# Two weight units interleaved at the start of a two-layer encoder kernel on one Trainium2 core

## The chip, the cores and the metric

The kernel runs on one core of one Trainium2 chip. The core has TensorE (PE, matrix products into PSUM), VectorE (DVE), ScalarE (ACT), GpSimd (POOL) and SyncE (SP, which here only issues transfers). The metric is the device time of one execution in microseconds. Three runs of the kernel before gave a median of 1763.88 us, from 1763.88 to 1764.26.

## The reference

The program is a two-layer encoder on 512 tokens of width 1024, everything in float32. For each layer it computes

```python
x = x + hybrid_mixer(rms_norm(x, norm_mix_g[l]), w_in[l], ...)        # 3 branches, gates, w_out
x = x + mem_cross_attention(rms_norm(x, norm_xattn_g[l]), mem, ...)
x = x + conv_ffn(rms_norm(x, norm_ffn_g[l]), w_up[l], ..., w_down[l])
```

and at the end one more `rms_norm`. The mixer multiplies the normed x by a wide `w_in`. Its first 1024 columns feed a branch that gates them (`a * sigmoid(b)`) and runs a causal convolution of 31 taps over them; other columns feed a differential attention and a gated branch, in which a causal 128x128 matrix `w_s` mixes tokens and a bias `b_s` is added. `rms_norm(x)` is `x * rsqrt(mean(x * x) + eps) * g`.

## The kernel before, in words

All activations lie transposed: 128 features on the partitions, 8 tiles of them (`KD`), 512 tokens along the free side. Every large product is done in split precision. A float32 operand is rounded to a "head" of TensorE's float32r type, and the "tail" is the operand minus its head. A product is then head*head + tail*head + head*tail, three matmuls of 128x128 by 128x512 for each block.

The weights come in "units" of 128x2048 floats (1 MB), 78 for a layer, laid out on the host in the order of use. A unit is loaded by SP into `raw[:, g % 2]`, its head is written by ACT (or for a few pieces by DVE) into `w_hd[:, g % 2]`, and its tail by POOL or DVE into `w_tl[:, g % 2]`. Two slots exist, so unit g + 2 waits for unit g. A unit of the kinds used first ("ab") holds 8 blocks of 256 columns, two output tiles (t = 0, 1) for each input tile `kc`. Its 48 matmuls collect in a pair of PSUM banks.

The order of the work is written out by hand, one program for each engine. An engine runs its list in order, and a counter for each engine (`line.done`, `line.at`) carries the waits between them. Labels name the steps: `n0_head{t}` and `n0_tail{t}` are the two parts of x tile t times the gain `g_mix`; `of_unit("head", g)`, `("tail", g)` are the parts of unit g; `("used", g)` says that `w_hd` of unit g was read, `("over", g)` that its last matmul was done; `ev{e}` says that DVE or ACT has emptied the PSUM banks of entry e.

The norm is not applied before the products. The gains are folded into x, and the factor of each token, `rsqrt(mean square)`, is multiplied in when the PSUM banks are emptied. So the first products can start before the norm is known. The factor is made like this: ACT squares the 8 tiles of x (`n0_sq{t}`) into `sq`, which has two places; DVE adds them up in `ssum` (`first_sum`, 7 additions in a row, the last labelled `n0_all`); PE turns `ssum` with 4 transposes (`turned_sums`); DVE reduces it and adds eps (`mean_square`, `n0_ms`); POOL takes the power -0.5 (`n0_rs`); PE spreads the result over the partitions with 4 transposes (`spread`, `n0b`); DVE copies it into `r0` (`n0_r`). In this order each addition waits for its square, and each square from the third on waits for the addition that frees its place.

At the start, PE first runs 14 matmuls on a tile of ones. Then it works through unit 0 in two halves of four input tiles (lines 1508, 1513 and 1522), then unit 1 (lines 1532, 1533 and 1542). Between the head matmuls of unit 1 and its 16 tail matmuls stand `first_sums`: 4 matmuls (lines 1418, 1419) that sum the columns of `w_s` for both layers, and the 4 transposes of `ssum` (line 1398). After unit 1 comes the spread (line 1406), then unit 2. POOL prepares `w_s` for those column sums: it masks it (line 573) and splits it into head and tail (lines 577, 579), after both `w_s` and `b_s` have landed. DVE uses the column sums in 8 small operations (line 997, `bs{lay}_{g}`).

The loads at the start are all issued by SP in one row: x tiles 0-1, first half of unit 0, x 2-3, second half of unit 0, x 4-5, x 6-7, unit 1, `w_st` (that is `w_s`), `b_s`, the other vectors, the identity.

## Time and profile of the kernel before

| what | value |
|---|---|
| median of 3 runs | 1763.88 us |
| the profiled execution, its own time | 1764.1 us |
| its span (first to last instruction) | 1762.3 us |
| PE busy | 1753.0 us, 99% |
| PE weight loads busy | 1452.8 us, 82% |
| DVE busy | 1244.2 us, 71% |
| ACT busy | 730.7 us, 41% |
| POOL busy | 483.7 us, 27% |
| granted TensorE clock over the span | 0.999 |
| the chain that ended last | 98% PE |

The profiled execution lies 1.8 us above its span, since something lies before the first and after the last instruction that is recorded. Busy shares are averages; the change touches only about the first 35 us, so what matters are rows of that stretch. Times in rows count from the start of the span.

### The profile page before, as it was taken

What the parts mean: (1) busy time and instruction counts of PE and PEld (TensorE: products, weight loads), DVE (VectorE), ACT (ScalarE), POOL (GpSimd) and SP (SyncE); (2) the same over time, 40 slices, a digit from 0 to 9 for tenths busy, and PEclk for the clock granted to TensorE, in tenths of its full rate; (3) what the DMA queues carried; (4) which work ended last, traced back from release to release, by engine and by line L of the source; (5) the groups of instructions that cost most, each with busy time, mean ns of one, the idle gap of its engine ahead of it and who ended that gap; (6) DMA issues with size and microseconds to landing.
All of it is one profiled execution on the core that took longest, in us unless ns stands there. A gap on an engine that the chain in (4) does not pass through costs nothing.

```text
span 1762.3 us, 21613 instructions
## 1 busy us (share of the span) xinstructions
PE 1753.0 (99%) x8152; PEld 1452.8 (82%) x8152; DVE 1244.2 (71%) x1656; ACT 730.7 (41%) x940; POOL 483.7 (27%) x201
## 2 busy tenths in 40 slices
PE   9999999999999999999999999999999999999998
PEld 7888888888878888888888888888888788888888
DVE  7987856563568786577779678555744797685586
ACT  5233644343464433343432246443444544343342
POOL 6453000103014244444133620010030232444440
PEclk9999999999999999999999999999999999999999
DMA  5532222322222322232332312223222223322322
GB/s 216 190 120 72 102 102 83 133 96 96 96 96 96 120 99 93 96 113 81 118 143 72 143 65 109 103 95 120 96 96 96 96 96 120 117 75 96 120 73 71
DMA packets 30120, 185.95 MB, mean 106 GB/s; under 512 B 3644, under 2 KB 5948, under 8 KB 9536
## 3 DMA queue, kind: packets, MB, share of 16 engines
q1 hardware_dynamic: 27804, 172.71, 27.4%
q0 software_dynamic: 1648, 11.54, 1.7%
q8 instruction: 64, 1.05, 0.2%
q10 hardware_dynamic: 564, 0.33, 0.1%
q14 instruction: 40, 0.33, 0.1%
HBM read 179.25 MB, written 7.68 MB: 106 GB/s over the span
## 4 chain that ended last, share of the span: by engine, by line
PE 98%; DVE 1%; DMA 1%; issue 0%; ACT 0%; SPq 0%; DVEq 0%; POOL 0%; ACTq 0%
PE ps L1542 28%; PE ps L1532 28%; PE ps L1533 28%; PE ps L1448 2%; PE ps L1440 2%; PE ps L1439 2%; PE ps L1570 1%; PE ps L1590 1%; PE ps L1622 1%; PE ps L1604 1%; DMA raw<-units 1%; DVE ssum L931 1%; PE ps L1582 0%; PE ps L1708 0%; PE ps L1714 0%; PE ps L1707 0%
## 5 line engine op out<-in xcount | busy, mean ns | idle before, releaser
L1532 PE MATMUL ps<-x_hd,w_hd 128*128 128x512 f32 x1584 | 619.5, 391 | 0.0
L1533 PE MATMUL ps<-x_tl,w_hd 128*128 128x512 f32 x1584 | 617.2, 390 | 0.0
L547 POOL TENSOR_TENSOR w_tl<-raw,w_hd 128x2048 fp32r<-128x2048 f32 x80 | 370.0, 4625 | 534.9 <-ACT w_hd L652 396.9
L652 ACT ACTIVATE w_hd<-raw 128x2048 fp32r<-128x2048 f32 (+1 forms) x156 | 298.4, 1913 | 343.2 <-PE ps L1533 258.9
L1542 PE MATMUL ps<-x_hd,w_tl 128*128 128x512 f32 x1584 | 377.3, 390 | 0.0
L1532 PEld LDWEIGHTS ps<-x_hd,w_hd 128*128 128x128 f32 x1584 | 297.4, 188 | 62.5 <-issue 0.3
L1533 PEld LDWEIGHTS ps<-x_tl,w_hd 128*128 128x128 f32 x1584 | 297.6, 188 | 61.1
L1542 PEld LDWEIGHTS ps<-x_hd,w_tl 128*128 128x128 f32 x1584 | 297.1, 188 | 61.5
L1532 PE MATMUL ps<-ring_hd,w_hd 128*128 128x512 f32 (+1 forms) x640 | 242.1, 382 | 0.0
L1533 PE MATMUL ps<-ring_tl,w_hd 128*128 128x512 f32 (+1 forms) x640 | 240.0, 379 | 0.0
L900 DVE TENSOR_TENSOR w_tl<-raw,w_hd 128x2048 fp32r<-128x2048 f32 x75 | 172.0, 2293 | 51.8 <-ACT w_hd L652 40.4
L1231 DVE SCALAR_TENSOR_TENSOR merged<-merged 128x512 f32<-128x512 f32 x44 | 183.0, 4160 | 21.3 <-ACT merged L652 20.9
L1097 DVE TENSOR_TENSOR resid<-resid,ps 128x512 f32<-128x512 f32 x120 | 77.1, 684 | 115.9 <-PE ps L1542 112.6
L1041 DVE SCALAR_TENSOR_TENSOR ps<-cg,pv_all,ps 128x512 f32<-128x512 f32 x232 | 154.5, 750 | 0.0
L1542 PE MATMUL ps<-ring_hd,w_tl 128*128 128x512 f32 (+1 forms) x640 | 151.5, 379 | 0.0
L1532 PEld LDWEIGHTS ps<-ring_hd,w_hd 128*128 128x128 f32 x640 | 120.3, 188 | 29.3 <-issue 4.3
L1533 PEld LDWEIGHTS ps<-ring_tl,w_hd 128*128 128x128 f32 x640 | 120.4, 188 | 22.7 <-issue 0.5
L1542 PEld LDWEIGHTS ps<-ring_hd,w_tl 128*128 128x128 f32 x640 | 116.0, 188 | 22.4
L652 ACT ACTIVATE ring_hd<-merged 128x512 fp32r<-128x512 f32 x44 | 27.9, 633 | 224.9 <-DVE merged L1233 224.9
L1222 DVE SCALAR_TENSOR_TENSOR merged<-tmp,pv_all,merged 128x510 f32<-128x510 f32 (+1 forms) x176 | 120.3, 745 | 0.9 <-ACT merged L652 0.9
L652 ACT ACTIVATE merged<-tmp,pv_all 128x512 f32<-128x512 f32 x88 | 71.9, 817 | 117.3 <-DVE tmp L1211 113.2
L1211 DVE TENSOR_TENSOR tmp<-ps,sq 128x512 f32<-128x512 f32 x88 | 56.7, 686 | 82.0 <-PE ps L1542 81.4
(198 smaller groups left out, 1522.0 us busy)
## 6 DMA issues: line engine op xcount, KB each, us to landing
raw<-units SPq DMA_DIRECT2D x155, 1024.0 KB, 4.8
resid<-x_t SPq DMA_DIRECT2D x4, 512.0 KB, 7.9
bias_t<-bias_tiles POOLq DMA_DIRECT2D x8, 256.0 KB, 5.3
cg<-mem_t POOLq DMA_DIRECT2D x2, 1024.0 KB, 6.3
resid<-x_t POOLq DMA_DIRECT2D x1, 2048.0 KB, 8.2
resid_dram<-resid POOLq DMA_DIRECT2D x1, 2048.0 KB, 7.5
resid<-resid_dram POOLq DMA_DIRECT2D x1, 2048.0 KB, 8.8
out<-resid SPq DMA_DIRECT2D x7, 256.0 KB, 2.3
```

The source lines that it names most:

```text
L547: line.done(pool.tensor_tensor(w_tl[:, k % 2, :], raw[:, k % 2, :], w_hd[:, k % 2, :].bitcast(F32), ALU.subtract), of_unit("tail", g))
L652: line.done(act.activation(out, in_, func, **kw), *labels)
L900: op(lambda: dve.tensor_tensor(w_tl[:, slot, :], raw[:, slot, :], w_hd[:, slot, :].bitcast(F32), ALU.subtract), of_unit("tail", g), needs= ...
L1041: op(lambda: dve.scalar_tensor_tensor(dst, src, w, acc, ALU.mult, ALU.add), independent=1)
L1097: op(lambda: dve.tensor_tensor(dst, dst, ps[:, banks(e) + i, :], ALU.add), f"{tag}_{j + i}", f"ev{e}", needs=(f"e{e}",), independent=i)
L1211: op(lambda: dve.tensor_tensor(src, ps[:, b + i, :], r_all, ALU.mult), f"up_src{arg}_{i}", f"ev{e}", needs=(f"e{e}",), independent=i)
L1222: op(lambda: dve.scalar_tensor_tensor(dst[:, sh:S], src[:, 0:S - sh], col(l, "ffn_w", 3 * c + 2 - sh), dst[:, sh:S], ALU.mult, ALU.add), f ...
L1231: op(lambda: dve.scalar_tensor_tensor(th, th, 1.0, ft[:, f0, :], ALU.add, ALU.mult), needs=(f"th_f{arg}",))
L1439: pe.matmul(ps[:, b + t, :], xh[:, kc, a], w, start=kc == 0, stop=False)
L1532: pe.matmul(dst, w_hd[:, slot, w], hd[:, src, :], start=kc == 0, stop=False)
L1533: i = pe.matmul(dst, w_hd[:, slot, w], tl[:, src, :], start=False, stop=False)
L1542: i = pe.matmul(dst, w_tl[:, slot, w], hd[:, src, :], start=False, stop=kc == nk - 1)
```

## The change

Units 0 and 1 are now worked on together. PE takes a pair of input tiles, does its 12 matmuls for unit 0 (4 head, 4 x-tail, 4 weight-tail) and the same for unit 1, then goes to the next pair. The very first tile of unit 0 is done alone. The loads are cut finer: x comes in five parts (tiles 0, 1, 2-3, 4-5, 6-7), each of the two units in three steps (512, 512 and 1024 columns), in the order of use. DVE now rounds all heads of unit 0, ACT all of unit 1, and DVE makes all six tails, each for one step. The squares of x go to the eight tiles of `merged`, so no square waits for an addition. The 14 matmuls on ones become 9. `first_sums` moves to the last pair of unit 0, with 16 matmuls of the two units behind it as before; the column sums of layer 1 use bank 6 in place of 5. The spread moves into unit 2, behind its first 8 matmuls. POOL's work on `w_s` waits for `w_st` alone, and `b_s` has a semaphore of its own.

PE from its first matmul, before:

```order
L1413 MATMUL ps<-ones 128x128 x14
L1508 MATMUL ps<-x_hd,w_hd 128x512 x4
L1513 MATMUL ps<-x_tl,w_hd 128x512 x4
L1508 MATMUL ps<-x_hd,w_hd 128x512 x4
L1513 MATMUL ps<-x_tl,w_hd 128x512 x4
L1522 MATMUL ps<-x_hd,w_tl 128x512 x8
```

PE from its first matmul, now (1566 multiplies heads, 1572 x tails, 1578 weight tails):

```order
L1451 MATMUL ps<-ones 128x128 x9
L1566 MATMUL ps<-x_hd,w_hd 128x512 x2
L1572 MATMUL ps<-x_tl,w_hd 128x512 x2
L1578 MATMUL ps<-x_hd,w_tl 128x512 x2
L1566 MATMUL ps<-x_hd,w_hd 128x512 x2
L1578 MATMUL ps<-x_hd,w_tl 128x512 x2
L1572 MATMUL ps<-x_tl,w_hd 128x512 x2
L1566 MATMUL ps<-x_hd,w_hd 128x512 x4
L1572 MATMUL ps<-x_tl,w_hd 128x512 x4
L1578 MATMUL ps<-x_hd,w_tl 128x512 x4
```

The first matmuls need one x tile and a quarter of unit 0; the last three rows are unit 1 with the same two x tiles.

PE around the sums and the spread, before (1418, 1419 are the column sums, 1398 turns `ssum`, 1406 spreads, 1532 on the last row is unit 2):

```order
L1418 MATMUL ps<-ring_hd,ones 128x512
L1419 MATMUL ps<-ring_tl,ones 128x512
L1418 MATMUL ps<-ring_hd,ones 128x512
L1419 MATMUL ps<-ring_tl,ones 128x512
L1398 MATMUL ps<-ident,ssum 128x128 x4
L1542 MATMUL ps<-x_hd,w_tl 128x512 x16
L1406 MATMUL ps<-ident,rs 128x128 x4
L1532 MATMUL ps<-x_hd,w_hd 128x512
```

The same place now (1542 and 1543 are unit 2, of whose 8 matmuls ahead of the spread the first two stand; the spread, line 1444, comes behind all 8):

```order
L1457 MATMUL ps<-ring_tl,ones 128x512
L1436 MATMUL ps<-ident,ssum 128x128 x4
L1578 MATMUL ps<-x_hd,w_tl 128x512 x4
L1566 MATMUL ps<-x_hd,w_hd 128x512 x4
L1572 MATMUL ps<-x_tl,w_hd 128x512 x4
L1578 MATMUL ps<-x_hd,w_tl 128x512 x4
L1542 MATMUL ps<-x_hd,w_hd 128x512
L1543 MATMUL ps<-x_tl,w_hd 128x512
```

The transposes of `ssum` have 16 matmuls behind them in both, but the spread has moved behind 8 more.

DVE from x tile 2 to the additions, before:

```order
L924 SCALAR_TENSOR_TENSOR x_tl<-resid,pv_all,x_hd 128x512 x2
L954 TENSOR_TENSOR w_tl<-raw,w_hd 128x1024
L924 SCALAR_TENSOR_TENSOR x_tl<-resid,pv_all,x_hd 128x512 x4
L954 TENSOR_TENSOR w_tl<-raw,w_hd 128x1024
L900 TENSOR_TENSOR w_tl<-raw,w_hd 128x2048
L931 TENSOR_TENSOR ssum<-sq 128x512
L931 TENSOR_TENSOR ssum<-ssum,sq 128x512 x6
```

DVE over the same stretch now:

```order
L952 SCALAR_TENSOR_TENSOR x_tl<-resid,pv_all,x_hd 128x512
L978 CAST w_hd<-raw 128x512
L952 SCALAR_TENSOR_TENSOR x_tl<-resid,pv_all,x_hd 128x512
L983 TENSOR_TENSOR w_tl<-raw,w_hd 128x512 x2
L952 SCALAR_TENSOR_TENSOR x_tl<-resid,pv_all,x_hd 128x512 x2
L978 CAST w_hd<-raw 128x1024
L983 TENSOR_TENSOR w_tl<-raw,w_hd 128x1024
L952 SCALAR_TENSOR_TENSOR x_tl<-resid,pv_all,x_hd 128x512 x2
L983 TENSOR_TENSOR w_tl<-raw,w_hd 128x1024
L960 TENSOR_TENSOR ssum<-merged 128x512
L960 TENSOR_TENSOR ssum<-ssum,merged 128x512 x6
```

The seven additions stand last in both lists, and ahead of them DVE has more and smaller pieces.

The diff, cut to its core:

```diff
-NORM_AT = (1, 0)
-X_PARTS = ((0, 2), (2, 4), (4, 6), (6, 8))
+NORM_AT = (0, 0)
+SPREAD_AT = (2, 1)
+X_PARTS = ((0, 1), (1, 2), (2, 4), (4, 6), (6, 8))
 PIECE = UNIT // 4
+SUMS_AT = (4, 6)
+STEPS = (slice(0, PIECE), slice(PIECE, 2 * PIECE), slice(2 * PIECE, UNIT))
...
+            def load_step(n, p):
+                done = weights_in[n] if p == 2 else piece_in[n][p]
+                sp.dma_start(raw[:, n, STEPS[p]], units[n][:, STEPS[p]]).then_inc(done, 16)
+
             load_x(0)
+            load_step(0, 0)
             load_x(1)
+            load_step(1, 0)
             load_x(2)
+            load_step(0, 1)
+            load_step(1, 1)
             load_x(3)
+            load_step(0, 2)
+            load_x(4)
+            load_step(1, 2)
             sp.dma_start(v_sb[:, 0:DEPTH, :], w_st).then_inc(ws_in, 16)
+            sp.dma_start(ident[:], ident_in).then_inc(ident_loaded, 16)
...
-                    pool.wait_ge(ws_in, 16 * 2)
+                    pool.wait_ge(ws_in, 16)
...
+            first_tiles((0, 1))
+            second_unit(0)
+            squares_of_x((0,))
+            first_tiles((2, 3))
+            second_unit(1)
+            squares_of_x((1, 2))
+            first_tiles((4, 5))
+            squares_of_x((3,))
+            first_tiles((6, 7))
+            second_unit(2)
+            squares_of_x((4, 5, 6, 7))
...
-            for _ in range(14):
+            for _ in range(9):
                 pe.matmul(ps[:, 5, 0:P], ones[:], ones[:], start=True, stop=True)
...
+                pe.wait_ge(vector_done, line.at("step_head0_0"))
+                heads(0, (0,))
+                rests(0, (0,))
+                tails(0, (0,), 0)
+                heads(0, (1,))
+                tails(0, (1,), 0)
+                rests(0, (1,))
+                for j in range(4):
+                    kcs, p = (2 * j, 2 * j + 1), min(j, 2)
+                    for n in (0, 1) if j else (1,):
+                        pe.wait_ge(scalar_done if n else vector_done, line.at(f"step_head{n}_{p}"))
+                        heads(n, kcs)
+                        i = rests(n, kcs)
+                        if j == 3:
+                            line.done(i, of_unit("used", n))
+                        if (j, n) == (3, 0):
+                            first_sums()
+                        i = tails(n, kcs, p)
+                        if j == 3:
+                            line.done(i, f"e{FIRST_OF[n]}", of_unit("over", n))
...
                     if g == 2:
-                        pe.wait_ge(vector_done, line.at(f"bs{DEPTH - 1}_3"))
+                        pe.wait_ge(vector_done, line.at("bs0_3"))
...
-                                first_spread if l and k == NORM_AT[l] + 1 else None)
+                                first_spread if k == SPREAD_AT[l] else None)
...
-                    if k == NORM_AT[l] and not l:
-                        first_spread()
```

`heads`, `rests` and `tails` each run over the input tiles `kcs` and both output tiles, waiting for `n0_head{kc}`, `n0_tail{kc}` and `step_tail{n}_{p}`. In layer 1 the sums and the spread stay where they were.

## Rows read from the trace of the kernel before

**Rows 1.** Waits of PE over the whole span, the longest: us in total, times, longest.

```profile
PE ps L1508 <- DVE w_hd L950: 1.2, 1, 1.2
```

**Rows 2.** Chain of waits, 0 to 80 us: start us, us, what.

```profile
17.28 2.30 DVE w_tl L900
19.68 0.95 DVE ssum L931
...
21.32 0.91 DVE ssum L931
22.33 1.61 DVE ssum L931
...
26.76 0.70 DVE ssum L931
...
28.30 0.66 PE ps L1398 x4
28.96 3.64 PE ps L1542 x16
32.60 0.44 PE ps L1406 x4
...
72.96 3.63 PE ps L1542 x16
```

**Rows 3.** Timeline of the start, PE: start us, us, engine, line, operation, [idle before].

```profile
1.09 4.98 PE L1413 MATMUL ps<-ones 128*128 128x128 f32 x28 [1.09 <-POOL ones L558]
...
7.31 1.19 PE L1508 MATMUL ps<-x_hd,w_hd 128*128 128x512 f32 x4 [1.23 <-DVE w_hd L950]
```

**Rows 4.** Timeline of the start, ACT and DVE.

```profile
5.13 1.54 ACT L652 ACTIVATE x_hd<-resid,pv_all 128x512 fp32r<-128x512 f32 x2 [1.77 <-DMA pv_all<-pvec]
...
6.82 0.43 DVE L950 CAST w_hd<-raw 128x512 fp32r<-128x512 f32 x1
...
8.67 1.54 ACT L652 ACTIVATE x_hd<-resid,pv_all 128x512 fp32r<-128x512 f32 x2 [2.01 <-DMA resid<-x_t]
...
11.10 1.22 DVE L954 TENSOR_TENSOR w_tl<-raw,w_hd 128x1024 fp32r<-128x1024 f32 x1
...
12.30 3.20 DVE L924 SCALAR_TENSOR_TENSOR x_tl<-resid,pv_all,x_hd 128x512 fp32r<-128x512 f32 x4
```

**Rows 5.** Timeline of the start, SP's issue of `w_st` and POOL's work on it.

```profile
4.67 0.66 SPq L476 DMA_DIRECT2D v_sb<-w_st  x1
...
17.88 3.24 POOL L573 TENSOR_SCALAR_AFFINE_SELECT v_sb<-v_sb 128x512 f32<-128x512 f32 x2 [2.98 <-DMA v_sb<-bs]
...
21.76 1.62 POOL L579 TENSOR_TENSOR ring_tl<-v_sb,ring_hd 128x512 fp32r<-128x512 f32 x1
...
24.48 1.62 POOL L579 TENSOR_TENSOR ring_tl<-v_sb,ring_hd 128x512 fp32r<-128x512 f32 x1
```

**Rows 6.** Transfers issued in 0 to 60 us: KB each, median us to landing.

```profile
v_sb<-w_st SPq DMA_DIRECT2D x1, 512.0 KB, 11.6
```

**Rows 7.** Groups of PE, 3.5 to 4 us, then 5.5 to 6.2 us: busy us, mean ns.

```profile
L1413 PE MATMUL ps<-ones 128*128 128x128 f32 x4 | 1.1, 421 | 0.0
...
L1413 PE MATMUL ps<-ones 128*128 128x128 f32 x6 | 0.8, 275 | 0.0
```

**Rows 8.** Timelines of DVE (28 to 100 us) and POOL (26 to 180 us).

```profile
33.07 0.69 DVE L1106 COPY r<-ps 128x512 f32<-128x512 f32 x1 [0.77 <-PE ps L1406]
...
38.13 4.37 DVE L1126 SCALAR_TENSOR_TENSOR cg<-tmp,cg 128x512 f32<-128x512 f32 x1
...
58.76 4.34 DVE L982 TENSOR_TENSOR bias_t<-bias_t 128x256 f32<-128x256 f32 x1
...
73.11 1.29 DVE L1130 TENSOR_TENSOR merged<-ps,r 128x512 f32<-128x512 f32 x2
...
37.34 4.61 POOL L547 TENSOR_TENSOR w_tl<-raw,w_hd 128x2048 fp32r<-128x2048 f32 x1 [1.26 <-ACT w_hd L652]
...
58.20 4.61 POOL L547 TENSOR_TENSOR w_tl<-raw,w_hd 128x2048 fp32r<-128x2048 f32 x1 [9.50 <-ACT w_hd L652]
```

More of the change, by code:

```diff
@@ L430, in build @@
         weights_in = [sem("weights_in0"), sem("weights_in1")]
-        half_in = sem("half_in")
+        piece_in = [[sem(f"piece_in{n}_{p}") for p in range(2)] for n in range(2)]
         x_in = [sem(f"x_in{n}") for n in range(len(X_PARTS))]
@@ L929, in first_sum @@
                 if t:
-                    first = sq[:, 0, :] if t == 1 else ssum[:]
-                    op(lambda: dve.tensor_tensor(ssum[:], first, sq[:, t % 2, :], ALU.add), (lay, f"{tag}_sum{t}"),
+                    square = sq[:, t % 2, :] if lay else merged[:, t, :]
+                    first = ssum[:] if t > 1 else sq[:, 0, :] if lay else merged[:, 0, :]
+                    op(lambda: dve.tensor_tensor(ssum[:], first, square, ALU.add), (lay, f"{tag}_sum{t}"),
                        *(((lay, f"{tag}_sum0"),) if t == 1 else ()), *(((lay, f"{tag}_all"),) if t == KD - 1 else ()),
@@ L991, in spatial_biases @@
             def spatial_biases():
-                dve.wait_ge(ws_in, 32)
+                dve.wait_ge(bs_in, 16)
                 for lay in range(DEPTH):
@@ L1417, in spatial_sums @@
                     pe.wait_ge(gpsimd_done, line.at(f"ws_mask{lay}"))
-                    pe.matmul(ps[:, 4 + lay, :], ones[:].bitcast(F32R), ring_hd[:, lay, :], start=True, stop=False)
-                    line.done(pe.matmul(ps[:, 4 + lay, :], ones[:].bitcast(F32R), ring_tl[:, lay, :], start=False,
+                    pe.matmul(ps[:, SUMS_AT[lay], :], ones[:].bitcast(F32R), ring_hd[:, lay, :], start=True, stop=False)
+                    line.done(pe.matmul(ps[:, SUMS_AT[lay], :], ones[:].bitcast(F32R), ring_tl[:, lay, :], start=False,
                                         stop=True), f"wsum{lay}")
@@ L1543, in product, with first_two_units, blocks, heads @@
                 return i
+            def first_two_units():
+                def blocks(n, kcs):
+                    for kc in kcs:
+                        for t in (0, 1):
+                            c = 256 * kc + P * t
+                            yield kc, slice(c, c + P), ps[:, banks(FIRST_OF[n]) + t, :]
+                def heads(n, kcs):
+                    for kc, w, dst in blocks(n, kcs):
+                        pe.wait_ge(scalar_done, line.at(f"n0_head{kc}"))
+                        i = pe.matmul(dst, w_hd[:, n, w], x_hd[:, kc, :], start=kc == 0, stop=False)
+                    return i
+                def rests(n, kcs):
+                    for kc, w, dst in blocks(n, kcs):
+                        pe.wait_ge(vector_done, line.at(f"n0_tail{kc}"))
+                        i = pe.matmul(dst, w_hd[:, n, w], x_tl[:, kc, :], start=False, stop=False)
+                    return i
+                def tails(n, kcs, p):
+                    pe.wait_ge(vector_done, line.at(f"step_tail{n}_{p}"))
+                    for kc, w, dst in blocks(n, kcs):
+                        i = pe.matmul(dst, w_tl[:, n, w], x_hd[:, kc, :], start=False, stop=kc == KD - 1)
+                    return i
+                pe.wait_ge(vector_done, line.at("step_head0_0"))
[18 more added lines that the diff above has]
+                            line.done(i, f"e{FIRST_OF[n]}", of_unit("over", n))
             def spatial(e, pair_arg):
```

108 lines of the change are left out of this document (46 added, 62 removed).

## The prediction, made before the changed kernel was run

> **What bounds the kernel now.** I read the page first, then PE's waits over the whole span, then the chain of waits through the first 80 us, then the timelines of the engines on that chain. The span is 1762.3 us, PE is busy for 1753.0 of it by the page, and the longest wait that PE has anywhere is 1.2 us, for the first rounded weights [rows 1]. So PE bounds everything, and the change can only move the moment at which PE is through with units 0 and 1. All later matmuls are the same in number and size.
>
> That moment is 33.04 us: the spread starts at 32.60 and takes 0.44 [rows 2]. PE's own work until there is short of the time. The first real matmul starts at 7.31 [rows 3]; 16 matmuls take 3.64 us, so 0.2275 each [rows 2], and the 96 of both units take 21.8. The 4 column sums (about 1.0 at the same pace), the turning (0.66) and the spread (0.44) make it 23.9. 33.04 - 7.31 = 25.7, so 1.8 us is idle, and 7.3 us lies ahead of the first matmul.
>
> What ends last at the place of the sums is not PE but DVE. The chain goes through the weight tail of unit 1 (ends at 19.58), then the seven additions of squares, from 19.68 to 28.26 [rows 2]; the row of 26.76 is 0.70 long, the next addition starts 0.80 later, and its end is 28.26. Then come 0.66 of turning, 3.64 of tails and the spread. An addition alone takes 0.70, but two take 1.61: the one of 22.33 ends at 23.94, and POOL's subtraction of 21.76 to 23.38 lay over it [rows 2, 5]. Further on the same is seen: an operation of DVE with two inputs in SBUF, started at 38.13 while POOL ran from 37.34 to 41.95, ended at 42.50; another, at 58.76 beside POOL's 58.20 to 62.81, ended at 63.10 [rows 8]. So DVE waits until POOL is through and needs some 0.3 to 0.6 us more. But the first addition, started at 19.68 in the middle of POOL's masking (17.88 to 21.12), was through in 0.95 [rows 2, 5], so the masking costs DVE 0.25 at most. The Trainium skill, SBUF — State Buffer, "Who interferes with whom", has one rule for all of it: the two share a port pair, one holds it for its whole instruction, and the other fully blocks. The trace agrees for the subtractions and not for the masking; by the rule alone the first addition would have ended after 21.12.
>
> **The change, part by part.**
>
> First matmul. ACT's first x head starts at 5.13, released by the gains, and takes about 0.72, since two take 1.54 [rows 4]. DVE can round the first quarter unit in 0.43 beside it. PE starts at about 5.95 instead of 7.31, 1.36 us earlier. Then it starves a little: weight tail and x tail of the first tile are there at 7.5 and 6.7, and ACT's head of unit 1 at about 7.4. I count 0.8 us of gaps until 10 us and none later, so PE reaches the sums after 80 matmuls: 5.95 + 18.2 + 0.8 = about 24.9. With the column sums it is ready to turn at 25.8. POOL's part of these is no longer late: `w_st` lands at 4.67 + 11.6 = 16.3 [rows 5, 6], POOL starts there and not at 17.88, and what ended at 24.48 + 1.62 = 26.1 [rows 5] ends at about 24.6.
>
> DVE's list up to the additions. Tiles 2-3 land behind 1.5 MB of transfers in both kernels, so I keep 8.6 us, as ACT's third head waits for it until 8.67 [rows 4]; DVE's tail of tile 2 starts at about 9.5. From there: six x tails at 0.80, as four take 3.20 [rows 4] (4.80), a rounding of 512 columns (0.43), one of 1024, which no row shows (bounds 0.43 and twice 0.43; I take 0.75), two weight tails of 512 and two of 1024 columns. A tail of 1024 is 1.22 and one of 2048 is 2.30 [rows 2, 4], so one of 512 is 0.69; with 0.1 between them that is 1.58 + 2.64. The sum is 10.2, and 9.5 + 10.2 = 19.7. DVE may also wait up to 0.4 for ACT's head of tile 4, since ACT now squares between the heads, but the roundings start without the 0.1 between. I take 19.7, with 20.1 as the upper end. Before, it was 19.68. This is the step on which the forecast rests: DVE does the same arithmetic on smaller pieces and starts the additions at the same moment.
>
> The additions. Seven at a pace of 0.80 are 5.6 us. Before they took 8.58, of which 0.70 was waiting for a square whose place was not free, since DVE stood idle from 20.63 to 21.32 after the first addition [rows 2]; that goes, because the squares now have eight places. The rest was POOL. Its four operations on the port (two roundings, two subtractions) still fall into this stretch, now from 19.6 to 24.6, and cost again 2 x 0.91 and about 2 x 0.22. 5.6 + 2.3 = 7.9, so the last ends at 27.6 instead of 28.26. PE waits from 25.8 to 27.6, and what it won at its start is gone there.
>
> From there: turning 0.66, 16 matmuls 3.64, and the spread, moved into unit 2, 0.44 all the same. The gain is 28.26 - 27.6 = 0.65 us.
>
> The cut transfers, 10 issues in place of 6 ahead of `w_st`, cost nothing if the bytes flow as before; SP issues one in 0.4 to 0.7, faster than they land. Fewer matmuls on ones cost nothing by themselves. The heads of unit 2 wait for `used` of unit 0, now at about 24.9; ACT needs 1.9 and PE wants them at about 32, so this is hidden. The spread moved behind 8 matmuls makes DVE's `r0` later: 27.65 + 0.66 + 3.64 + 1.82 + 0.44 = 34.2 against 33.07 [rows 8]. Behind it the emptying of all banks is queued. PE asks for that first where it is tight at unit 6, at 72.96 + 3.63 = 76.59 [rows 2]; DVE is through with the banks at 73.11 + 1.29 = 74.40 [rows 8], so there are 2.2 us. The lag of 1.2 fits even if nothing absorbs it; and it mostly is absorbed, since the operation of 58.76 ends when POOL lets it, at 63.1, wherever it begins.
>
> Sum: 0.65 us less. Against the profiled execution (1764.1) that is 1763.45, against the median of the runs, 0.2 lower, 1763.2.
>
> **The rivals.**
>
> A, the additions are not last. If DVE gets to them a microsecond earlier, or POOL's operations miss them, they end by 25.8 and PE never waits. For it: the gaps on PE are few and 1.8 us of contention is a matter of which instruction starts first. Against it: DVE's 10.2 us are a plain sum, and the additions alone end at 25.3 only if POOL costs nothing. Then the second unit ends at 25.8 + 0.66 + 3.64 + 0.44 = 30.5, 2.5 us less than 33.04: 1761.4. Chance 0.17, with intermediate gains of 1.2 to 2.5.
>
> B, smaller transfers land later. The Trainium skill, DMA: Bandwidth & Descriptors, "Measured (HBM→SBUF, 128 partitions, SWDGE, issued from GpSimd)", has the rule to batch transfers to 1 MB or more, and 256 KB would be far below. By rows, tiles 2-3 at 8.6 us set DVE's start; each 0.5 us later moves the additions by 0.5, so the gain is gone at 0.65 us and at 1 us it is 0.35 slower: 1764.2. Against it: several are in flight together, and ten issues of up to 0.66 us are no slower than the bytes. Chance 0.15.
>
> B2, the masking blocks after all. It now starts at 16.3, beside DVE's x tails and weight tails, which have two inputs in SBUF. If the x tail of about 16.9 had to wait for the masking's end at 19.5, all behind it would be 2.6 later; four of POOL's operations would then be half over, which gives back about 1. Net 1.6 - 0.65 = 1.0 slower, 1764.9. Against it is the first addition of before, above. It is the page's rule of the port pair, taken at its word. Chance 0.03.
>
> C, slower: the clock of TensorE. In the matmuls on ones a matmul takes 421 ns until 4 us and 275 ns after 5.5 [rows 7], while the profile gives a granted clock of 0.999 over the whole span; so PE seems to start at the lower level (1.2 GHz) and to rise while the matmuls on ones run, from 1.09 to 6.07 [rows 3]. With 9 of 14 they end near 4.8, and PE then stands for 1.1 us and goes on with gaps. If the rise fails to come there, matmuls of 512 columns take up to twice 0.2275 until it does. The wait of 1.8 us at the turning covers 8 of them, and the 0.8 of gaps 3 more; with the forecast's 0.65 it decides from about 14 matmuls at the lower level. If it lasts for the 24 matmuls of the first pair, that is 24 x 0.2275 = 5.5 - 2.6 - 0.65 = 2.2 us slower, 1766.1. [...] Chance 0.08.
>
> D, the late `r0` bites: one more full collision with POOL of 4.37 - 0.70 = 3.7 us between 34 and 58 us that is not absorbed makes a lag of 4.9 against 2.2 of room plus 0.65: 3.3 us of waiting at unit 6, net 2.7 slower, 1766.6. For it: POOL's unit tails are 4.6 us long. Against it: the collision of 38.13 is already there and the next at 58.76 absorbs. Chance 0.05.
>
> **How the numbers follow.** My forecast, 1763.2 with its own range of 1762.6 to 1763.8, has a chance of 0.52; A 0.17, B 0.15, B2 0.03, C 0.08, D 0.05. The 80% range takes in all of B and B2, most of A on the one side, and the smaller forms of C on the other: 1761.4 to 1765.4. What a measurement can tell here from no change is about 0.2%, or 3.5 us. Faster by that would need all of A and 1 us more, below 1760.4: 0.03. Slower by it, above 1767.4, needs C or D beyond the prices given: 0.04. Within it: 0.93.
>
> **What would show it.** Right: in the profile after, PE's first real matmul is near 6 us; the first addition starts near 19.7 and the last ends near 27.6, with two of 1.6 beside POOL's subtractions; PE waits 1 to 2 us for `ssum` before line 1436; unit 2 starts near 31.9; nothing waits at unit 6. Wrong: no wait at line 1436 (A); ACT's third x head released later than 9 us (B); matmuls of over 500 ns behind 6 us (C); PE waiting for DVE near 75 us (D).

## The result and the profile after

| kernel | median us | runs | lowest to highest |
|---|---|---|---|
| before | 1764.02 | 22 | 1763.81 to 1764.31 |
| after | 1767.03 | 22 | 1764.77 to 1768.72 |

After to before: ratio 1.0016, 95% interval 1.001 to 1.0022. The change makes the kernel 3.0 us slower, and its runs spread over 4.0 us where those of before spread over 0.5. The profiled execution after took 1765.92 us with a span of 1764.2; before it was 1764.1 and 1762.3 [table of the profile before]. So this one execution shows 1.9 us of the loss, and the median holds 1.1 more. The two parts turned out to have different causes.

Waits of PE over the whole span, after (us in total, times, longest); they answer to [rows 1]:

```profile
PE ps L1436 <- DVE ssum L960: 3.0, 1, 3.0
```

Before, the longest was 1.2 us, at the first weights. Now one of 3.0 us stands ahead of the turning of `ssum` (line 1436), where 1.8 was forecast.

Chain of waits, after, 0 to 45 us (start us, us, what); it answers to [rows 2]:

```profile
2.66 7.87 DMA resid<-x_t
10.55 0.73 ACT x_hd L664
...
22.32 1.61 DVE ssum L960
...
29.12 0.70 DVE ssum L960
29.86 0.66 PE ps L1436 x4
30.52 0.94 PE ps L1578 x4
...
41.92 3.17 PE ps L1552 x14
```

Read it from the top. The part of the chain shown begins with one transfer, x tiles 2-3, which is through at 10.53. Before, ACT had that tile at 8.67 [rows 4]. From there ACT or DVE is at work all the time until the additions, which start at 22.32 and not at 19.68 [rows 2], and end at 29.82. PE then does in 0.66 and 16 matmuls what it did before. Unit 2's weight tails start at 41.92; before they started at 40.32:

```profile
40.32 3.63 PE ps L1542 x16
```

So 1.60 of the 1.9 us arises here. The rest arises far behind: the same kind of rows lie 1.65 us later than before at 1399 us and 2.01 later at 1475 us. What happens between them is not shown.

Timelines of SP's queue, DVE and POOL, after (start us, us, engine, line, operation, [idle before]); it answers to [rows 4, 5]:

```profile
4.22 1.55 SPq L471 DMA_DIRECT2D resid<-x_t  x1
...
8.40 0.67 SPq L488 DMA_DIRECT2D v_sb<-w_st  x1
```

```profile
11.31 0.75 DVE L952 SCALAR_TENSOR_TENSOR x_tl<-resid,pv_all,x_hd 128x512 fp32r<-128x512 f32 x1 [2.11 <-ACT x_hd L664]
...
17.27 1.23 DVE L983 TENSOR_TENSOR w_tl<-raw,w_hd 128x1024 fp32r<-128x1024 f32 x1
18.41 2.26 DVE L952 SCALAR_TENSOR_TENSOR x_tl<-resid,pv_all,x_hd 128x512 fp32r<-128x512 f32 x2
20.77 1.45 DVE L983 TENSOR_TENSOR w_tl<-raw,w_hd 128x1024 fp32r<-128x1024 f32 x1
...
24.02 5.79 DVE L960 TENSOR_TENSOR ssum<-ssum,merged 128x512 f32<-128x512 f32 x6
```

```profile
18.45 1.68 POOL L585 TENSOR_SCALAR_AFFINE_SELECT v_sb<-v_sb 128x512 f32<-128x512 f32 x2 [7.67 <-DMA v_sb<-w_st]
...
24.47 1.60 POOL L591 TENSOR_TENSOR ring_tl<-v_sb,ring_hd 128x512 fp32r<-128x512 f32 x1
```

Three things are seen. DVE's list starts 1.8 us late (11.31 against the 9.5 of the prediction). Its last x tails and weight tail are longer beside POOL than a moment before: two x tails take 2.26 where two alone take 1.6, and the weight tail 1.45 where the one of 17.27 took 1.23. And `w_st` is issued only at 8.40, not at 4.67 [rows 5]: 11 issues of SP stand ahead of it in place of 7, and one of them takes 1.55 us.

Traffic from 8 to 9 us (the columns are the stretch, its length, the busy time of PE, PEld, DVE, ACT and POOL, the granted clock, the DMA share and GB/s), before and then after:

```profile
8.00:9.00 1.00, 1.00 (x6) 0.81 (x5) 0.53 (x2) 0.33 (x1) 1.00 (x6) 1.00 1.01 414
```

```profile
8.00:9.00 1.00, 1.00 (x6) 0.81 (x5) 0.90 (x2) 0.96 (x2) 1.00 (x3) 1.00 0.99 254
```

The DMA engines are full in both (share about 1), but after they move 254 GB/s in place of 414, and in the next microsecond 311 in place of 426. The cut transfers hold 2 KB for each partition (256 KB each), the uncut ones 4 KB or more. That looks like a price of the small transfers, but the experiments below show that this stretch is not the place to read it.

There is a second difference. The transfer of x tiles 2-3 is issued at another time, and it takes another time to land (SP's issue, then KB and us from issue to landing; before, then after):

```profile
1.71 0.43 SPq L467 DMA_DIRECT2D resid<-x_t  x1
resid<-x_t SPq DMA_DIRECT2D x1, 512.0 KB, 6.9
```

```profile
2.66 0.43 SPq L471 DMA_DIRECT2D resid<-x_t  x1
resid<-x_t SPq DMA_DIRECT2D x1, 512.0 KB, 7.9
```

Four issues stand ahead of it in place of two, so it is issued 0.95 us later, and then it needs 1.0 us more. Together these are the 1.9 us.

### The profile page after: what moved, and what is told of

It reads as the page before. It is cut to its first block, busy times and chain, and to the rows that moved or that the text cites. A ratio compares the mean times of both kernels' runs of the same rounds, so it can differ in the third digit from the quotient of the medians.

```text
span 1764.2 us, 21606 instructions
## 1 busy us (share of the span) xinstructions
PE 1752.1 (99%) x8142; PEld 1451.7 (82%) x8142; DVE 1242.4 (70%) x1660; ACT 729.9 (41%) x941; POOL 481.1 (27%) x201
## 3 DMA queue, kind: packets, MB, share of 16 engines
q1 hardware_dynamic: 28380, 172.71, 27.6%
## 4 chain that ended last, share of the span: by engine, by line
PE 97%; DVE 1%; DMA 0%; issue 0%; ACT 0%; SPq 0%; DVEq 0%; POOL 0%; ACTq 0%
PE ps L1542 28%; PE ps L1552 28%; PE ps L1543 28%; PE ps L1486 2%; PE ps L1478 2%; PE ps L1477 2%; PE ps L1627 1%; PE ps L1647 1%; PE ps L1679 1%; PE ps L1661 1%; DVE ssum L960 1%; PE ps L1639 0%; DMA resid<-x_t 0%; PE ps L1766 0%; PE ps L1772 0%; PE ps L1765 0%
## 5 line engine op out<-in xcount | busy, mean ns | idle before, releaser
L1552 PE MATMUL ps<-x_hd,w_tl 128*128 128x512 f32 x1568 | 373.5, 390 | 0.0
```

The costliest lines, as they stand in the source:

```text
L1552: i = pe.matmul(dst, w_tl[:, slot, w], hd[:, src, :], start=False, stop=kc == nk - 1)
```

## The experiments

Thirteen kernels were run, 11 times each, beside the kernel before on the same chip (medians 1763.99 to 1764.11). Two causes were on trial first: the small transfers make the tiles late (rival B of the prediction), or too few matmuls on ones cost clock (rival C). The stand of 3.0 us came in as a third after the first four runs. All differences here are 0.2% or less, so the 95% intervals of neighbouring kernels overlap; the readings rest on the traces and on how the 11 runs lie.

### Is it the number of matmuls on ones?

```diff
 a_warm14 (after)              b_warm9 (before)
-            for _ in range(9):         -            for _ in range(14):
+            for _ in range(14):        +            for _ in range(9):
```

> The changed kernel with 14 matmuls on ones at the start again, in place of 9; nothing else differs. Clock theory (with 9 the TensorE clock rises late, or falls again, in some executions, and that makes them up to 4 us apart): the runs lie together within 0.6 us as those of the kernel before do, near the fast end of the changed kernel, 1765 to 1766. Transfer theory (x tiles 2-3 land 1.9 us later and all behind them is late, and that is all): no change, median near 1767 and runs still 3 to 4 us apart.

> The kernel before with 9 matmuls on ones in place of 14. Clock theory: some executions get the full clock late, the runs lie 2 to 4 us apart and their median is 1765 to 1767. Otherwise: 1764.0 within 0.6 us like the kernel before, since PE's first real work waits for transfers until 7.3 us in both.

Measured: a_warm14 1766.64 (1764.48 to 1768.68), as wide as the kernel after and 0.4 below its median. b_warm9 1764.13 (1763.86 to 1765.14), 0.1 above before. So the number of ones explains at most a small part of the 3.0 us. But a_warm14's profiled execution (1767.4) caught what the one of after had missed. Its chain from the turning:

```profile
29.83 0.76 PE ps L1436 x4
30.59 1.71 PE ps L1578 x4
32.30 1.61 PE ps L1566 x4
```

The first eight matmuls behind the stand of 3.0 us take 3.3 us, where after's take 1.86. The clock column says why (same columns as above), a_warm14 and then after:

```profile
30.00:32.00 2.00, 2.00 (x8) 1.71 (x8) 1.72 (x7) 0.00 (x0) 0.17 (x1) 0.56 0.00 0
```

```profile
30.00:32.00 2.00, 2.00 (x12) 1.69 (x12) 1.72 (x7) 0.00 (x0) 0.15 (x1) 1.00 0.00 0
```

A granted clock near 0.5 is the lower level (1.2 GHz of 2.4); 0.56 is a mean of 2 us, most of them at the lower level. Its unit 2 reaches the weight tails at 43.47, 1.55 later than in the profile after. So PE stands 3.0 us in both executions, and in one of them the clock falls. The 22 runs of the kernel after point the same way: the four slowest, 1767.96 and above, are the ones with the lowest granted clock over the span, 0.997.

### Is it the stand?

```diff
 a_fill (after)
                     spatial_sums()
+                    for _ in range(13):
+                        pe.matmul(ps[:, 5, 0:P], ones[:], ones[:], start=True, stop=True)
                 turned_sums("n0")
```

> The changed kernel with 13 matmuls on ones (some 2.8 us at full clock) between the column sums and the turning of the sum of squares, where PE stood idle for 3.0 us in the profile of the changed kernel. They give nothing that is used. Theory 'stand': the idle 3 us make the TensorE clock fall to its lower level in most executions, for a stretch that differs from one to the next, and that is what sets the runs 4 us apart; then the runs here lie within 1 us and at the fast end, 1764.8 to 1765.8, median 1765.4 or so, so 1.5 us faster than the changed kernel. Theory 'landing': the transfers land at different times from run to run; then the spread of 4 us stays and the median is near 1767.

Measured: 1765.79 (1765.09 to 1766.28), ratio to before 1.0009 (1.0001 to 1.0018). PE turns at 29.96, 0.1 later than in the kernel after, behind matmuls on ones that fill the place of the wait:

```profile
27.06 3.06 PE L1698 MATMUL ps<-ones 128*128 128x128 f32 x26
29.96 0.60 PE L1436 MATMUL ps<-ident,ssum 128*128 128x128 f32 x4
```

Nothing was made earlier (unit 2's weight tails start at 41.92 again), and 1.2 us of the median came back, with the spread down from 4.0 to 1.2 us. The interval overlaps that of the kernel after (1.001 to 1.0022); it is the spread that speaks. So the second part of the loss is the clock behind the stand: 1.55 us in the one execution caught at the lower level, more or less in others.

### Is it the size of the transfers?

```diff
 b_rows2k (before)
-X_PARTS = ((0, 2), (2, 4), (4, 6), (6, 8))
+X_PARTS = ((0, 1), (1, 2), (2, 4), (4, 6), (6, 8))
 ... unit 0 and unit 1 loaded as 512 + 512 + 1024 columns
```

> The kernel before, with the work in its old order, but x tiles 0 and 1 apart and the first two quarters of units 0 and 1 apart, so in rows of 2 KB. Transfer theory: ACT's head of tile 2 starts 1.5 to 2 us later than 8.67, the additions and all behind them are 1 to 1.6 us late, and the time is 1764.8 to 1765.6 in all runs within 0.6 us. If the rows cost nothing: 1764.0. Clock theory says nothing of it, the 14 matmuls are there.

```diff
 a_rows4k (after)
-X_PARTS = ((0, 1), (1, 2), (2, 4), (4, 6), (6, 8))
+X_PARTS = ((0, 2), (2, 4), (4, 6), (6, 8))
 ... the first two steps of each unit loaded as one transfer of 1024 columns, issued in the order x01, unit 0, x23, unit 1, x45, ...
```

> The changed kernel with its interleaved work, but with first transfers of 512 KB in rows of 4 KB for each partition (x in four parts, each unit in two halves, in the order x 0-1, unit 0a, x 2-3, unit 1a, x 4-5, unit 0b, x 6-7, unit 1b). Transfer theory (rows of 2 KB move at some 250 to 300 GB/s where rows of 4 KB move at over 400): here x 2-3 lands near 8.6 us as before, the last addition ends 1.5 to 2 us earlier than in the changed kernel, near 28, and the fastest run is near 1763.2; the first matmul comes at 7.3 again. Clock theory: the runs still lie 3 to 4 us apart, since the 9 matmuls on ones are kept, and with a longer stand behind them (4.8 to 7.3 us) perhaps further.

b_rows2k: 1765.07 (1764.57 to 1765.6), 1.0 above before; ratio 1.0006 (0.9997 to 1.0015), so the interval just takes in no change, but the time is as expected. ACT's third head is 1.0 late against [rows 4], and so is the turning behind the additions (28.30 before, [rows 2]):

```profile
9.69 1.54 ACT L659 ACTIVATE x_hd<-resid,pv_all 128x512 fp32r<-128x512 f32 x2 [1.76 <-DMA resid<-x_t]
```

```profile
7.15 8.94 DMA raw<-units
...
29.30 0.66 PE ps L1407 x4
```

The second fence is from the chain of waits, and in this order the chain does not go through x tiles 2-3. It goes through the last piece of unit 1, issued at 7.1 and through at 16.09; before, unit 1 was issued at 4.01 and through at 15.24. So the run shows that the cut costs 1.0 us, by all that it delays, and not by this one tile.

Where does the delay come from? The traces of five kernels side by side; landing is the time of issue plus the time from issue to landing, and the rates are means over the stretch:

| kernel | smallest first transfers | x 2-3 issued, landed (us) | GB/s, 1 to 8 us | GB/s, 8 to 10 us |
|---|---|---|---|---|
| before | 512 KB | 1.71, 8.6 | 258 | 420 |
| after | 256 KB | 2.66, 10.5 | 231 | 283 |
| b_rows2k | 256 KB | 2.66, 9.7 | 220 | 404 |
| a_rows4k | 512 KB | 1.71, 8.5 | 269 | 272 |
| a_order (below) | 512 KB | 1.71, 8.9 | 259 | 346 |

From 8 to 10 us the rate does not follow the size: a_rows4k, with nothing cut to 2 KB for a partition, is as slow as the kernel after, and b_rows2k is nearly as fast as before. From 1 to 8 us it does, 220 to 231 against 258 to 269. And in both cut kernels x 2-3 is issued 0.95 us later. In b_rows2k it then lands 7.0 us after its issue, as before (6.9), so the tile's delay there is as long as the later issue alone. In the kernel after it needs 7.9. For unit 1 of b_rows2k the flow is the nearer cause: 38 GB/s less over 7 us is 0.27 MB, by estimate 0.65 us at the 405 GB/s of 10 to 18 us, of the 0.85 by which it is late. Slower flow and later issue come together wherever the transfers were cut, and no run separates them for x 2-3; why it is 0.9 us later in the kernel after than in b_rows2k is open too.

a_rows4k: 1767.13 (1767.03 to 1767.35), no gain, against what I expected, though x 2-3 was there at 8.5. ACT works its list in order, and with whole halves the second unit's first head is not there in time. ACT waits for it until 10.34, with x tiles 2-3 behind it until 11.73:

```profile
10.34 0.63 ACT L662 ACTIVATE w_hd<-raw 128x512 fp32r<-128x512 f32 x1 [3.63 <-DMA raw<-units]
```

So with whole halves the interleaved order makes ACT and DVE wait for more bytes. A second version asks for unit 1 later in ACT's and DVE's lists.

```diff
 a_order (a_rows4k with another order of loads and lists; PE as it was)
-            load_x(2)
             load_step(0, 2)
+            load_x(2)
 ...
             first_tiles((0, 1))
-            second_unit(0)
-            squares_of_x((0,))
+            squares_of_x((0, 1))
             first_tiles((2, 3))
+            second_unit(0)
             second_unit(1)
 ...
             first_tail(0, 1)
-            tail_of_step(1, 0)
-            first_tail(0, 2)
             round_step(1)
-            first_tail(0, 3)
+            first_tail(0, 2)
             tail_of_step(0, 1)
+            first_tail(0, 3)
+            tail_of_step(1, 0)
```

> The changed kernel with all first transfers in rows of 4 KB and no engine asked for unit 1 before it is there: loads x 0-1, unit 0a, x 2-3, unit 1a, unit 0b, x 4-5, x 6-7, unit 1b; ACT's list has x tiles 0 to 3 ahead of the pieces of unit 1, PE does two pairs of unit 0, two of unit 1, then alternates. Theory 'transfers and order': x 2-3 at 8.6 us, the last addition ends at 27.8 to 28.5, PE stands for under 1.5 us, no loss of clock: 1763.4 to 1764.4, runs within 0.5 us. If the interleave itself costs, for example since DVE's small tail pieces run into POOL's masking: 1765 or more.

Measured: 1765.65 (1765.52 to 1765.84), ratio 1.0009 (1.0 to 1.0018): 1.4 us less than after, and a spread of 0.3. ACT has tiles 2-3 at 8.94, nearly as before, and PE stands only 1.0 us at the turning. But the additions still start at 23.29:

```profile
17.24 4.39 DVE L950 SCALAR_TENSOR_TENSOR x_tl<-resid,pv_all,x_hd 128x512 fp32r<-128x512 f32 x2
21.74 1.44 DVE L981 TENSOR_TENSOR w_tl<-raw,w_hd 128x1024 fp32r<-128x1024 f32 x1
23.29 1.59 DVE L958 TENSOR_TENSOR ssum<-merged 128x512 f32<-128x512 f32 x1
24.98 4.67 DVE L958 TENSOR_TENSOR ssum<-ssum,merged 128x512 f32<-128x512 f32 x6
```

Two x tails take 4.39 where they need 1.5. POOL works from 17.59 to 24.34 without a rest:

```profile
17.59 1.23 POOL L583 TENSOR_SCALAR_AFFINE_SELECT v_sb<-v_sb 128x512 f32<-128x512 f32 x2
18.78 0.60 POOL L587 CAST ring_hd<-v_sb 128x512 fp32r<-128x512 f32 x1
19.46 1.63 POOL L589 TENSOR_TENSOR ring_tl<-v_sb,ring_hd 128x512 fp32r<-128x512 f32 x1
...
22.19 2.15 POOL L589 TENSOR_TENSOR ring_tl<-v_sb,ring_hd 128x512 fp32r<-128x512 f32 x1
```

### Is it POOL?

```diff
 a_order_pool (a_order)
                     pool.wait_ge(ws_in, 16)
+                    pool.wait_ge(vector_done, line.at("step_tail1_2"))
```

> The kernel after with transfers of 512 KB in a better order, and POOL's work on w_s (masking, rounding, subtraction) held back until DVE's last weight tail. Theory: POOL beside the x tails and weight tails is what made DVE's list end at 23.2 us with the transfers in time; without POOL there it ends near 21.3 us, all of POOL's work then lies beside the additions, they take 8.5 us and more as before (end 29.8 to 30.5), and the column sums come later still. So the first addition starts 1.5 to 2 us earlier than 23.29 and the last ends no earlier than 29.5: the time is that of the ordered version, 1765.2 to 1766.5. Rival: DVE's list is long by itself and POOL cost it nothing: the first addition starts at 23.0 or later. Second rival: the additions are slowed only by subtractions, 3.7 us; then they end at about 28.5 and the time is 1 us less.

Measured: 1764.65 (1764.31 to 1765.54), ratio 1.0004 (0.9995 to 1.0012), 1.0 us less than a_order. DVE's rows at the same place:

```profile
17.36 1.41 DVE L951 SCALAR_TENSOR_TENSOR x_tl<-resid,pv_all,x_hd 128x512 fp32r<-128x512 f32 x2
18.87 1.23 DVE L982 TENSOR_TENSOR w_tl<-raw,w_hd 128x1024 fp32r<-128x1024 f32 x1
20.20 0.69 DVE L959 TENSOR_TENSOR ssum<-merged 128x512 f32<-128x512 f32 x1
21.00 7.40 DVE L959 TENSOR_TENSOR ssum<-ssum,merged 128x512 f32<-128x512 f32 x6
```

The same three operations that took 6.05 us (17.24 to 23.29) take 2.84 without POOL. The additions then take 8.20 in place of 6.36. Against 5.6 for seven alone, POOL costs DVE 3.2 + 0.8 = 4.0 us in a_order and 2.6 here; the work of POOL is the same. I had expected the end to stay at 29.5 or later and the time at 1765.2 or above; the second rival on record, 28.5 and 1 us less, came true. The additions ended at 28.40. Held back until DVE's tails are done, POOL's work meets the additions alone, and the same work costs DVE 1.4 us less: what a collision costs depends here on which operations meet, and not only on POOL's busy time.

The Trainium skill, SBUF — State Buffer, "Who interferes with whom", has this rule: DVE with two inputs in SBUF and GpSimd share a port pair, and who comes second is blocked for the whole instruction. In a_order the first of the two x tails is recorded from 17.24 to 19.93, the second so:

```profile
19.85 1.79 DVE x_tl L950
```

POOL's rounding ended at 19.38 and its subtraction at 21.09, so each x tail was through about 0.55 us behind the end of an instruction of POOL. That agrees with the rule for the second. The first had started at 17.24, ahead of the masking, and the masking and the rounding still went past it; which instruction held the ports when is not in the trace. Before, an addition was through in 0.95 in the middle of the masking [rows 2, 5].

### Is it the eight places of the squares?

```diff
 b_eight (before)
-                op(sq[:, t % 2, :], resid[:, t, :], ACT.Square, ...
-                   after + (((lay, f"{tag}_sum{t - 2}"),) if t >= 2 else ()))
+                place = sq[:, t % 2, :] if lay else merged[:, t, :]
+                op(place, resid[:, t, :], ACT.Square, ...
+                   after + (((lay, f"{tag}_sum{t - 2}"),) if t >= 2 and lay else ()))
```

> The kernel before with one part of the change alone: the squares of x of layer 0 go to the eight tiles of merged, so no square waits for an addition. My step: 0.70 us of waiting ahead of the second addition goes, POOL's operations on the port cost what they did, so 0.5 to 0.7 us less, 1763.4 in all runs. Rival: the additions only run into POOL's subtractions earlier and gain nothing, 1764.0.

Measured: 1763.88 (1763.7 to 1764.0), ratio 0.9999 (0.999 to 1.0007). The wait is gone, but only half of its 0.7 us with it: the additions take 8.22 instead of 8.58, from 19.81 (19.68 before) to 28.03 instead of 28.26. The rest turned into time beside POOL. And more would not have helped, since here PE's own work ends last. The chain runs through its column sums, the last of them from 27.90, straight into the turning:

```profile
19.81 0.94 DVE L933 TENSOR_TENSOR ssum<-merged 128x512 f32<-128x512 f32 x1
20.86 7.17 DVE L933 TENSOR_TENSOR ssum<-ssum,merged 128x512 f32<-128x512 f32 x6
```

```profile
28.14 0.60 PE ps L1400 x4
```

So in the kernel before DVE ended last at this place by only about 0.2 us, and the forecast of 0.5 to 0.7 less left out that PE itself is not ready before 28.1 in the old order. What the 0.7 would be worth in the new order, where PE is ready earlier, this run can't say.

### The clock at the start, and its cover

The first 8 real matmuls of a_order_pool and of b_warm9 were slow too (the expectation below says 12; in a_order_pool a pair takes 0.85 to 1.02 us from 6.92 to 10.58, and 0.46 from 11.13 on). The clock column there, of b_warm9, a_order_pool and the kernel after:

```profile
9.00:11.00 2.00, 2.00 (x6) 1.54 (x6) 1.37 (x2) 1.82 (x3) 2.00 (x11) 0.50 1.03 377
```

```profile
9.00:11.00 2.00, 2.00 (x7) 1.57 (x6) 1.76 (x4) 1.75 (x3) 2.00 (x7) 0.56 1.03 334
```

```profile
9.00:11.00 2.00, 2.00 (x11) 1.65 (x10) 0.19 (x1) 0.45 (x1) 1.77 (x13) 1.00 0.96 305
```

All three have 9 matmuls on ones. PE stood 2.6 us behind them in b_warm9 and 2.2 in a_order_pool, and 1.15 in the kernel after. The column can miss it: a_best_pool (below) stood 1.7 us, its column says 1.00 from 7 to 11 us, and still its second pair starts only 1.02 us after the first:

```profile
6.99 1.22 PE L1565 MATMUL ps<-x_hd,w_hd 128*128 128x512 f32 x2 [1.69 <-DVE w_hd L977]
```

So a_order_pool might owe part of its time to the clock.

```diff
 a_turn14 (a_order_pool), a_bp14 (a_best_pool, below)
-            for _ in range(9):
+            for _ in range(14):
```

> The ordered version with POOL's work held back (1764.65, first 12 real matmuls at the lower level, no wait at the turning, additions end at 28.40), with 14 matmuls on ones in place of 9. Theory: PE then stands for less than 1 us ahead of its first real matmul, which comes at 6.9 to 7.0, and all real matmuls run at 0.2275 us; PE gets ready to turn near 26.7 instead of 28.46, and there it waits 1.7 us for the additions, so that the time stays the same: 1764.2 to 1764.9. What ends last is then DVE's additions beside POOL, as in the kernel before. Rival: the slow start is not due to the row of ones; the first matmuls stay at 0.4 to 0.5 us each and nothing waits. Rival 2: the additions get earlier too, because fewer collisions remain, and the time falls by more than 1 us.

Measured: 1764.29 (1764.23 to 1765.05), ratio 1.0002 (0.9993 to 1.0011). All real matmuls run at the full pace behind a stand of 1.3 us:

```profile
7.82 0.73 PE L1565 MATMUL ps<-x_hd,w_hd 128*128 128x512 f32 x2 [1.29 <-DVE w_hd L977]
...
27.77 0.50 PE L1455 MATMUL ps<-ring_hd,ones 128*128 128x512 f32 x1 [0.46 <-POOL ring_tl L590]
```

The time is in the forecast, the path is not: I had the first matmul at 6.9 and a wait of 1.7 for the additions. It came at 7.82, and PE waited 0.46 for POOL's tail of `w_s`. PE turns at 28.34 against 28.46. In both it waits for POOL's tail (from 27.77 and from 27.90), and the additions end just then too (28.27 and 28.40), so the slow clock of a_order_pool lay in slack.

### Is there a version that beats both?

```diff
 a_late (after)
-                        if (j, n) == (3, 0):
-                            first_sums()              # sums of w_s and turning behind 80 matmuls
+                        if (j, n) == (3, 0):
+                            spatial_sums((0,))        # layer 0's sum alone
 ...
+                first_sums()                          # turning behind all 96
 ...
 spread and layer 1's sum behind 16 matmuls of unit 2
```

> The changed kernel with the turning of the sum of squares behind all matmuls of units 0 and 1, so 16 matmuls (3.6 us) stand where PE stood idle; the column sums of layer 1 and the spread come behind the first 16 matmuls of unit 2 (both column sums in bank 6). Theory 'stand': PE loses neither the 3.0 us nor the clock: unit 2 starts at about 30.8 and the time is 1761.8 to 1763, runs within 1 us, faster than both kernels. Rival: the factor r0 comes 2 us later still for DVE, and PE waits at unit 6 for emptied banks: 1763 to 1765, with a wait of 1 to 2 us on DVE near 75 us.

> The kernel after with transfers of 512 KB in a better order, and the turning of ssum behind all 96 matmuls of the two units, the column sums of layer 1 and the spread inside unit 2. The late turning alone gave 1764.05 and the ordering alone 1765.65, against 1767.0 for the kernel after and 1764.0 for the kernel before. If the two gains add up (each removes part of the stand of PE ahead of the turning) it would be 1762.7 to 1763.3. Rival: the late turning already removed the stand, so the earlier additions give nothing more, and what is left is what PE loses before them: 1763.8 to 1764.3. In the profile the second shows as PE's first matmul of unit 3 at the same moment as with the late turning alone.

> The same, and POOL's work on w_s held back until DVE's last weight tail. DVE's tails are then not held up by POOL's masking, but the column sums need POOL's result at about 29 us, and the additions run beside POOL and end at about 30: PE turns them at about 30 after 96 matmuls end at about 29.3. Expected 0 to 0.7 us above the version without the hold. If DVE's tails were what PE waits for before the turning, it is 0.5 to 1 us faster instead.

> The ordered version with POOL held back and the late turning (1765.4, unit 2's weight tails at 39.61, a wait of 0.8 at unit 6), with 14 matmuls on ones. Theory: PE loses 1.9 us less at the start and waits for the additions nowhere; the column sums of layer 0 want POOL's result at about 25 us, which is just there; unit 2's weight tails start at about 37.8 and the time is 1.0 to 1.9 us less, 1763.5 to 1764.4, if the wait at unit 6 does not grow. Rival: DVE's queue behind r0 bounds unit 6; r0 comes 1.9 us earlier too, but POOL's unit tails set when DVE is through, so that the wait at unit 6 grows to 1.5 to 2.7 us and the time stays at 1765.

a_best is a_order with a_late's turning; a_best_pool adds POOL's hold, a_bp14 the 14 ones.

| kernel | median (lowest to highest) | ratio to before |
|---|---|---|
| a_late | 1764.05 (1762.76 to 1764.79) | 0.9999 (0.999 to 1.0008) |
| a_best | 1765.64 (1764.77 to 1766.19) | 1.0007 (0.9999 to 1.0016) |
| a_best_pool | 1765.4 (1764.75 to 1766.21) | 1.0007 (0.9998 to 1.0016) |
| a_bp14 | 1764.13 (1763.85 to 1764.5) | 1.0 (0.9991 to 1.0009) |

None beats the kernel before. a_late takes back all of the 3.0 us, since PE no longer stands at the sums: its transposes come at 29.40, when 96 matmuls are done. The 1761.8 to 1763 hoped for did not come; the rival on record did, a new wait of 1 to 2 us at unit 6, and its chain is the way of the prediction's rival D:

```profile
PE ps L1477 <- DVE merged L1168: 1.2, 1, 1.2
```

```profile
35.87 0.70 DVE r L1144
...
74.80 0.69 DVE merged L1168
```

`r0` is there 2.8 us later than before (33.07, [rows 8]), and DVE's queue behind it is full until unit 6 (one operation there takes 4.50 us, from 40.81). In the kernel after this does not show: its `r0` comes at 36.49, but PE is 1.6 us late itself and never waits there.

a_best missed its forecast (1762.7 to 1763.3, or 1763.8 to 1764.3 by its rival). a_best_pool came out 0.2 below a_best, where 0 to 0.7 above it or 0.5 to 1 below was expected. Both have 9 ones and stand 2.5 and 1.7 us behind them, with slow first matmuls; with 14 ones, a_bp14 is 1.3 us faster than a_best_pool (forecast: 1.0 to 1.9), with its wait at unit 6 unchanged at 0.8.

## Why the prediction was wrong, step by step

**What bounds the kernel: right.** PE bounds it and only its time at units 0 and 1 moves; 1.60 of 1.9 us of the profiled loss lies there.

**First matmul: right.** Forecast 5.95, measured 5.99. The 9 matmuls on ones (18 in the rows, where each counts twice) end at 4.84, and the matmuls behind them run at full pace.

**"Tiles 2-3 land behind 1.5 MB of transfers in both kernels, so I keep 8.6 us": wrong, and together with "cost nothing if the bytes flow as before", said of the cut transfers, the step that failed.** The place in the row of bytes stayed the same, but the landing did not: the tiles were issued at 2.66 instead of 1.71 and landed 7.9 us later instead of 6.9, so ACT had them at 10.55 and not at 8.67. From 1 to 8 us 231 GB/s flowed in place of 258. B had this mechanism, priced at 1764.2 for 1 us; it was 1.9, and B's own rule (each 0.5 us moves the additions by 0.5) would have given about 1765.1. B took the later issue for harmless ("no slower than the bytes"); in b_rows2k, with the same cut in the old order, the delay of this tile is as long as the later issue alone. The Trainium skill, DMA: Bandwidth & Descriptors, "Measured (HBM→SBUF, 128 partitions, SWDGE, issued from GpSimd)", wants 1 MB or more in a transfer. The runs agree in direction for 256 against 512 KB, on transfers issued by SP, only from 1 to 8 us (220 to 231 against 256 to 269 GB/s over all kernels run), and the later issue stands beside it unseparated.

**DVE's list is 10.2 us long: 0.8 short.** It took 11.31 to 22.32, 11.0 us. The last two x tails and the weight tail behind them lost 0.9 beside POOL, and DVE waited 0.34 for ACT's head of tile 4, which the prediction had as its upper end; other terms were a little too high. Without POOL, a_order_pool takes 2.84 for the last three operations. "The masking costs DVE 0.25 at most" was read from one addition of before, and rival B2, at 0.03, was under-rated: in a_order the same x tails lost 2.9 us beside the masking and what follows it.

**"`w_st` lands at 4.67 + 11.6": wrong.** 4.67 is the issue before; with four more transfers ahead (11 in place of 7; the prediction counts 10 and 6) it moved to 8.40. It landed at 18.4 and POOL was through at 26.1, not 24.6.

**The 0.70 of waiting goes: in the old order 0.36 of it did** (b_eight, 8.22 against 8.58), and 0.2 reached the time.

**The additions, 7.9 us: 7.5.** From 22.32 they end at 29.82, 2.2 later than forecast and 1.56 later than before. Whether a start at 19.7 would have given the forecast 27.6 is not shown; no run put them there with POOL's work at this place. The prediction also let POOL's operations cost the same at any place, against which a_order and a_order_pool stand (4.0 and 2.6 us).

**The wait of 1 to 2 us before line 1436: it was 3.0,** and this is what made the second part of the loss. PE was ready 1.0 us later than forecast, at 26.85, and DVE 2.2 later. The prediction used such a wait as cover ("The wait of 1.8 us at the turning covers 8 of them") and did not ask what the wait itself does to the clock. Rival C had the clock, but put it at the ones (0.08, 1766.1). a_warm14 speaks against that place, a_fill and the clock column of a_warm14 show the other.

**Unit 6: right for the kernel after,** with no wait there. D's path became real only in a_late.

The sum, profiled: +1.8 landing and +0.8 in DVE's list, so that the additions start 2.64 later than before; they then take 7.50 instead of 8.58, -1.08. That is 1.56, and unit 2 moved by 1.60. On the median comes the clock, 1.2 by a_fill. The forecast had 0 for the landing, 0 for the list, -0.65 for the additions and 0 for the clock.

## What to carry to other kernels

Before you cut first transfers finer, look for the tile that the slowest chain waits for, and ask when that one lands; here the first matmul came 1.3 us earlier and the tile that counted 1.9 us later. Ask also when it is issued: each transfer put ahead of it cost about 0.47 us of SP's time here. A wait of the matrix engine that you add or lengthen can be priced twice: its length, here 3.0 us, and the matmuls behind it at the lower clock, here 1.55 us in one execution. A profile of one execution can miss this, so look at the spread of the runs. And where two engines slow each other, moving work of one of them moves the collision; here its price changed with the operations it met, from 4.0 to 2.6 us.

## What the runs showed of the hardware

- The clock fell in some executions and not in others of one kernel shape: behind a stand of 3.0 us not in after's profile, but to 0.56 in a_warm14's. At the start, behind 9 ones, it was 0.50 to 0.58 after stands of 2.6 and 2.2 us and 1.00 after 1.15; after 1.7 us (a_rows4k, a_best_pool) the matmuls were as slow although the column says 1.00. Behind 14 ones and 1.3 us it was 1.00. Whether the number of ones matters beside the length of the stand is open.
- An issue on SP's queue took 0.39 to 0.43 us for the first five, but up to 1.55 once several transfers were under way.
- With the first transfers cut to 2 KB for a partition, 220 to 231 GB/s flowed from 1 to 8 us, against 256 to 269 with 4 KB or more. From 8 to 10 us the rate went from 272 to 420 in kernels with nothing cut, with the engines' share full in all, so a full share says little about the rate. Only one cut was tried (512 columns); in b_rows2k it cost 1.0 us, not 1.9, and why the kernel after lost more is not shown.
